# Sample states, outputs and attention scores in alternating strips of the TensorE array; the last LayerNorm passes of the first FFN in the retention heads

## The reference

```
x = LN1(alpha*x + 0.5*SwiGLU_1(x))
q_a,k_a,v_a,q_r,k_r,v_r,g_r,gate_a,gate_b = split(x @ w_in)
A = windowed attention (128), 8 query heads of 64 in groups of 4 on 2 kv heads, rotary, a sink for each head
R = retention, 4 heads, keys 128, values 256, in chunks of 128:
    o = ((q k^T) * decay_mask) v + (q * q_decay) S ;  S = S * chunk_decay + (k * k_decay)^T v
    group norm of o, times silu(g_r)
x = LN2(alpha*x + (sigmoid(gate_a)*(A @ w_br_attn) + sigmoid(gate_b)*(R @ w_br_ret)) @ w_o)
x = LN3(alpha*x + 0.5*SwiGLU_2(x))
```

## Time and profile before

| | |
|---|---|
| median of 3 runs | 2530.76 us (2530.70 to 2531.70) |
| profiled execution | 2532.04 us, span 2530.1 us |
| PE busy | 2465.7 us (97%) |
| DVE / ACT / POOL busy | 65% / 36% / 9% |
| mean granted clock of TensorE | 0.988 |
| first FFN | to about 745 us |
| mixer groups 0, 1, 2 | from 745, 1081 and 1412 us on |
| second FFN | from about 1766 us on |

### The profile page before, as it was taken

One profiled execution on the slowest core, in us unless ns is written; L12 is line 12 of the kernel. 1 busy time (PEld: TensorE's weight loads), 2 busy tenths in 40 slices (PEclk: granted clock), 3 DMA queues, 4 the chain that ended last, 5 costly groups with the idle time before them and its releaser, 6 DMA issues.

```text
span 2530.1 us, 31985 instructions
## 1 busy us (share of the span) xinstructions
PE 2465.7 (97%) x12781; PEld 2103.9 (83%) x12781; DVE 1656.1 (65%) x2253; ACT 903.5 (36%) x1280; POOL 239.1 (9%) x306
## 2 busy tenths in 40 slices
PE   7999999999999999999999999999799999999997
PEld 6888888887888999988989778887688888888886
DVE  5666565557886657676576755566765656565788
ACT  4222222243443337433265322272422222223344
POOL 3000000000121100040000311200300000000011
PEclk9999999999999999999999999999899999999999
DMA  4232222276444333333332435434122222226643
GB/s 139 84 119 81 100 83 97 84 232 197 150 131 125 109 108 90 108 117 109 109 105 92 136 110 163 147 99 142 55 79 101 84 95 80 99 88 227 205 146 125
DMA packets 225603, 300.22 MB, mean 119 GB/s; under 512 B 13392, under 2 KB 166272, under 8 KB 222624
## 3 DMA queue, kind: packets, MB, share of 16 engines
q1 hardware_dynamic: 211792, 240.43, 30.2%
q0 software_dynamic: 13088, 56.61, 6.0%
q10 hardware_dynamic: 576, 1.15, 0.1%
HBM read 243.94 MB, written 55.18 MB: 118 GB/s over the span
## 4 chain that ended last, share of the span: by engine, by line
PE 88%; DVE 6%; ACT 2%; issue 2%; POOL 1%; DMA 1%; SPq 0%; DVEq 0%; ACTq 0%; POOLq 0%
PE ps L1804 25%; PE ps L1805 25%; PE ps L1806 25%; PE ps L1860 2%; PE ps L1859 2%; PE ps L2204 1%; PE ps L1940 1%; PE ps L1941 1%; PE ps L1868 1%; DVE w_lo L445 1%; PE ps L2099 1%; PE ps L2226 1%; PE ps L2105 1%; DVE b_lo L1253 1%; ACT w_hi L439 1%
## 5 line engine op out<-in xcount | busy, mean ns | idle before, releaser
L1804 PE MATMUL ps<-xc_hi,u_hi 128*128 128x512 f32 x1232 | 484.2, 393 | 0.0
L1805 PE MATMUL ps<-xc_lo,u_hi 128*128 128x512 f32 x1232 | 481.5, 391 | 0.0
L1806 PE MATMUL ps<-xc_hi,u_lo 128*128 128x512 f32 x1232 | 480.9, 390 | 0.0
L445 DVE TENSOR_TENSOR w_lo<-raw,w_hi 128x1024 fp32r<-128x1024 f32 x198 | 253.8, 1295 | 138.9 <-ACT w_hi L439 138.7
L1806 PEld LDWEIGHTS ps<-xc_hi,u_lo 128*128 128x128 f32 x1232 | 232.1, 188 | 49.5
L1804 PEld LDWEIGHTS ps<-xc_hi,u_hi 128*128 128x128 f32 x1232 | 232.6, 189 | 46.1
L1805 PEld LDWEIGHTS ps<-xc_lo,u_hi 128*128 128x128 f32 x1232 | 232.6, 189 | 45.2
L439 ACT ACTIVATE w_hi<-raw 128x1024 fp32r<-128x1024 f32 x198 | 205.6, 1054 | 170.1 <-PE ps L1806 146.6
L1804 PE MATMUL ps<-w_hi,xg_hi 128*128 128x512 f32 (+1 forms) x720 | 247.0, 343 | 1.7 <-issue 1.7
L1804 PE MATMUL ps<-b_hi,h_hi 128*128 128x512 f32 x616 | 241.8, 393 | 3.0 <-DVE b_lo L1253 3.0
L1805 PE MATMUL ps<-w_lo,xg_hi 128*128 128x512 f32 (+1 forms) x720 | 242.6, 337 | 0.0
(11 more groups left out here) (289 smaller groups left out, 4512.6 us busy)
## 6 DMA issues: line engine op xcount, KB each, us to landing
raw<-in_w_in SPq DMA_DIRECT2D x90, 512.0 KB, 3.8
wa<-in_ffn_wi SPq DMA_DIRECT2D x88, 512.0 KB, 3.5
h_raw<-h_spill SPq DMA_DIRECT2D x154, 256.0 KB, 2.8
h_spill<-tm POOLq DMA_DIRECT2D x22, 1024.0 KB, 4.1
b_raw<-in_ffn_wo SPq DMA_DIRECT2D x66, 256.0 KB, 3.8
raw<-in_w_in SPq DMA_DIRECT2D x96, 128.0 KB, 2.3
raw<-in_w_in SPq DMA_DIRECT2D x48, 256.0 KB, 3.0
raw<-in_w_br_ret SPq DMA_DIRECT2D x24, 512.0 KB, 3.4
```

Of the source, the lines that this page charges most:

```text
L445: nc.vector.tensor_tensor(wslot(n, True), raw[:, s * D:(s + 1) * D], fr(wslot(n, False)), ALU.subtract).then_inc(lo_ready, 1)
L1804: mm(out, a_hi, b_hi, start=first, stop=False)
L1805: mm(out, a_hi, b_lo, start=False, stop=False)
L1806: return mm(out, a_lo, b_hi, start=False, stop=last)
```

## The change

1. AS: a unit is now (token tile, half h of the query heads): 2 query heads of each kv head. Its 4 matmuls alternate between rows 0 to 63 (kv head 0, bank 3) and rows 64 to 127 (kv head 1, bank 4) of the array. The sinks are ordered to fit. AV's matmuls are ordered so that neighbours write the two halves of the partitions.
2. PVQ of the sample: qT_m has 4 copies instead of 8 (copy j keeps sequences j and j + 4). L2105 becomes 8 matmuls with 32 columns of weights each, alternating between PSUM partitions 0 to 31 (sequence j) and 32 to 63 (sequence j + 4).
3. SUa, SUb: kdec_m has 4 copies, made by one instruction. Each half is 4 matmuls with K = 32 rows, alternating between rows 0 to 31 (sequences 0 to 3, bank 6) and rows 32 to 63 (sequences 4 to 7, bank 7). The halves are now sequences 0, 1, 4, 5 and 2, 3, 6, 7, and the update of `st` reads and writes in that order.
4. The scale and shift of tiles 8, 4, 5 ahead of the mixer loop and of 6 and 7 in it are gone from there; DVE does tiles 8 and 4 at P 1, tiles 5 and 6 at P 2 and tile 7 at P 3 of group 0, behind the w_lo of that step and ahead of its rope.

```diff
@@ units_of
-    return [(t, n) for t in range(3 if G < NG - 1 else 2) for n in range(HKV)]
+    return [(t, h) for t in range(3 if G < NG - 1 else 2) for h in range(GQ // 2)]
@@ DVE, behind FFN 1
-            for t in (NT - 1, 4):
-                affine_scale(0, t)
-                affine_shift(0, t)
             pace.upto(MSLOTS + 1)
-            affine_scale(0, 5)
-            affine_shift(0, 5)
@@ DVE, mixer loop, behind pace.stage(n, k)
-                if G == 0 and kind == "G" and x == 1:
-                    affine_scale(0, 6)
-                elif G == 0 and kind == "G" and x == 2:
-                    affine_shift(0, 6)
-                elif G == 0 and kind == "G" and x == 3:
-                    affine_scale(0, 7)
-                elif G == 0 and kind == "GB" and x == 0:
-                    affine_shift(0, 7)
+                if G == 0 and (kind, x) in (("P", 1), ("P", 2), ("P", 3)):
+                    for t in ((NT - 1, 4), (5, 6), (7,))[x - 1]:
+                        affine_scale(0, t)
+                        affine_shift(0, t)
@@ DVE, PVQ
-                        for half in range(2):
-                            tt(kdec_m[0:SR, half * 4 * DK:(half + 1) * 4 * DK].rearrange("p (b c) -> p b c", b=4),
...
+                        tt(kdec_m[0:SR, 0:4 * DK].rearrange("p (b c) -> p b c", b=4),
...
@@ DVE, SUa and SUb
-                    sl = st[:, half * 4 * DV:(half + 1) * 4 * DV]
+                    sl = st[:].rearrange("p (r h c) -> p h r c", r=2, h=2)[:, half]
...
@@ PE, PVQ
-                            for b in range(DB):
-                                ins = mm(out, qT_m[:, b * SR:(b + 1) * SR], st[:, b * DV:(b + 1) * DV], start=False, stop=(b == DB - 1))
+                            for j in range(4):
+                                for r in range(2):
+                                    b, cols = 4 * r + j, j * SR + 32 * r
+                                    ins = mm(out[32 * r:32 * r + 32], qT_m[:, cols:cols + 32], st[:, b * DV:(b + 1) * DV],
+                                             start=False, stop=(j == 3))
@@ PE, SUa and SUb
-                    for b in range(4):
-                        kb = (4 * half + b) * DK
-                        ins = mm(ps[:, 6 * BANK + b * DV:6 * BANK + (b + 1) * DV], kdec_m[0:SR, kb:kb + DK],
-                                 v_r[0:SR, vb + 2 * DV:vb + 3 * DV], start=True, stop=True)
+                    for b in range(2):
+                        kb = (2 * half + b) * DK
+                        for r in range(2):
+                            rows = slice(32 * r, 32 * r + 32)
+                            ins = mm(bank(6 + r, P, b * DV, DV), kdec_m[rows, kb:kb + DK], v_r[rows, vb + 2 * DV:vb + 3 * DV],
+                                     start=True, stop=True)
@@ PE, AS
-                    for q in range(GQ):
-                        ins = mm(ps[:, 3 * BANK + q * 256:3 * BANK + (q + 1) * 256],
-                                 qaT[pr, t * 512 + q * P:t * 512 + (q + 1) * P], kaT[pr, t * P:(t + 2) * P], start=True, stop=True)
+                    for par in range(2):
+                        for nkv in range(HKV):
+                            pr = slice(nkv * HD, (nkv + 1) * HD)
+                            q = 2 * h + par
+                            ins = mm(bank(3 + nkv, P, par * 256, 256), qaT[pr, t * 512 + q * P:t * 512 + (q + 1) * P],
+                                     kaT[pr, t * P:(t + 2) * P], start=True, stop=True)
@@ PE, AV
-                    for q in range(GQ):
-                        r0 = (q % 2) * HD
...
+                    for nkv in range(HKV):
                         for s in range(2):
...
+                            for par in range(2):
...
```

More of the change, by code:

```diff
@@ L1559, in _ @@
                     dve.wait_ge(qkT_ready, 2 * g + 1)
-                    tt(qT_m[:].rearrange("p (b c) -> p b c", b=DB),
-                       qT[:, 2 * P:2 * P + SR].unsqueeze(1).to_broadcast([P, DB, SR]),
-                       batch_cols[:].rearrange("p (b c) -> p b c", b=DB), ALU.mult).then_inc(qTm_ready, 1)
+                    tt(qT_m[:, 0:4 * SR].rearrange("p (b c) -> p b c", b=4),
+                       qT[:, 2 * P:2 * P + SR].unsqueeze(1).to_broadcast([P, 4, SR]),
+                       batch_cols[:, 0:4 * SR].rearrange("p (b c) -> p b c", b=4), ALU.mult).then_inc(qTm_ready, 1)
                 elif kind == "SKV":
@@ L1597, in _ @@
                         dve.wait_ge(kdec_ready, g + 1)
-                        for half in range(2):
-                            tt(kdec_m[0:SR, half * 4 * DK:(half + 1) * 4 * DK].rearrange("p (b c) -> p b c", b=4),
-                               kdec[0:SR, (3 * (g % 2) + 2) * DK:(3 * (g % 2) + 3) * DK].unsqueeze(1).to_broadcast([SR, 4, DK]),
-                               batch_rows[0:SR, 4 * half:4 * half + 4].unsqueeze(2).to_broadcast([SR, 4, DK]),
-                               ALU.mult).then_inc(kdm_ready, 1)
+                        tt(kdec_m[0:SR, 0:4 * DK].rearrange("p (b c) -> p b c", b=4),
+                           kdec[0:SR, (3 * (g % 2) + 2) * DK:(3 * (g % 2) + 3) * DK].unsqueeze(1).to_broadcast([SR, 4, DK]),
+                           batch_rows[0:SR, 0:4].unsqueeze(2).to_broadcast([SR, 4, DK]), ALU.mult).then_inc(kdm_ready, 2)
                     dve.wait_ge(o_ready, g + 1)
@@ L1696, in _ @@
                     if kind == "AS":
-                        t, nkv = units_of(G)[x]
+                        t, h = units_of(G)[x]
                         msk = att_mask[:, 256:512] if (G or t) else att_mask[:, 0:256]
@@ L2216, in _ @@
                 elif kind == "AV":
-                    t, nkv = units_of(G)[x]
+                    t, h = units_of(G)[x]
                     u = len(units_of(0)) * G + x
                     pe.wait_ge(pT_ready, u + 1)
-                    if nkv == 0 and 3 * G + t:
+                    if h == 0 and 3 * G + t:
                         pe.wait_ge(oa_lo_ready, 3 * G + t)
-                    for q in range(GQ):
-                        r0 = (q % 2) * HD
-                        out = ps[r0:r0 + HD, 2 * BANK + (2 * nkv + q // 2) * P:2 * BANK + (2 * nkv + q // 2 + 1) * P]
+                    for nkv in range(HKV):
                         for s in range(2):
-                            ins = mm(out, va[:, (t + s) * P + nkv * HD:(t + s) * P + (nkv + 1) * HD],
-                                     probT[:, (2 * q + s) * P:(2 * q + s + 1) * P], start=(s == 0), stop=(s == 1))
+                            for par in range(2):
+                                j = 2 * nkv + par
+                                out = ps[par * HD:(par + 1) * HD, 2 * BANK + (2 * nkv + h) * P:2 * BANK + (2 * nkv + h + 1) * P]
+                                ins = mm(out, va[:, (t + s) * P + nkv * HD:(t + s) * P + (nkv + 1) * HD],
+                                         probT[:, (2 * j + s) * P:(2 * j + s + 1) * P], start=(s == 0), stop=(s == 1))
                     ins.then_inc(av_done, 1)
@@ L2381, in shape_constants @@
     c["att_mask_s"] = ms.reshape(P, 384).astype(f4)
-    onehot = (b[None, :] == np.arange(DB)[:, None]).astype(f4)
-    c["batch_cols"] = np.ascontiguousarray(np.broadcast_to(onehot.reshape(1, -1), (P, DB * SR)))
-    c["batch_rows"] = np.ascontiguousarray(onehot.T)
+    onehot = (b[None, :] % 4 == np.arange(4)[:, None]).astype(f4)
+    c["batch_cols"] = np.ascontiguousarray(np.broadcast_to(onehot.reshape(1, -1), (P, 4 * SR)))
+    c["batch_rows"] = np.ascontiguousarray(np.tile((b[:, None] % 4 == np.arange(4)[None, :]).astype(f4), (1, 2)))
     return c
@@ L2409 @@
     sk = np.asarray(inputs["attn_sinks"])[0]
-    consts["sinks"] = np.ascontiguousarray(np.broadcast_to(sk[None, :], (P, HQ)))
+    by_unit = sk.reshape(HKV, GQ // 2, 2).transpose(1, 0, 2).reshape(1, HQ)
+    consts["sinks"] = np.ascontiguousarray(np.broadcast_to(by_unit, (P, HQ)))
     consts["sinks_s"] = np.ascontiguousarray(np.tile(np.repeat(sk.reshape(HKV, GQ).T, DT, axis=0), (4, 1)))
```

6 lines of the change are left out of this document (3 added, 3 removed).

## The result

The changed kernel takes 2506.88 us (median of 4 runs, 2506.64 to 2511.54), the kernel before 2530.73 us beside it: 0.9906 of it, 95% interval 0.9894 to 0.9919, 23.9 us less. Timed once more beside other runs of before it was 0.9910 (0.9895 to 0.9925). The forecast was 13.0 us less, 2517.8, with a range from 2506 to 2526.

The account below looks back on a forecast made before the run. TensorE, busy 97% of the span, was taken to bound the kernel. Retention minus 12.6, attention minus 7.2, LayerNorm passes net plus 1.7 and clock plus 5.1 gave minus 13.0 us: 2530.8 to 2517.8, range 2506 to 2526.

Parts of the forecast that it names:

- Strips of rows and columns overlap two at a time: On PE, AS and SU go from 8 steps to 4, minus 0.84 us; L2105 from 16 to 8, minus 1.68 us.
- (b): Rival: strict program order, only one matmul's second record overlaps its neighbour's first; 2521 us, chance 0.08.
- (c): Rival: row strips don't overlap when weights are 128 wide, column strips do; AS and SU give nothing; 2529 us, chance 0.06.
- (d): Rival: no strip overlaps in these shapes; 2536 us, chance 0.03.
- Retention: Last group's sample outputs and state update: 13.4 us saved, less 0.84 us that becomes SUb 3's wait; minus 12.6 us.
- Attention: AS strips in three groups: ACT takes over as bound, so minus 7.2 us of 13.4 stays.
- LayerNorm passes, first half: Six DVE passes leave the place ahead of the first rope: minus 4.2 us of wait, minus 1.7 of clock; minus 5.9 us.
- LayerNorm passes, second half: Passes ahead of rope in P 1 to P 3 delay TR, T 0 and racc; plus 7.6 us, bounds 0 and 10.
- the old places ... give nothing back: Tile 6's and 7's passes lay beside POOL's rstd, 1.51 us of DVE's wait; leaving there gains nothing.
- Clock: Half clock behind new or longer waits of PE: plus 5.1 us, bounds 0 and 12.
- the seven waits: New or longer waits of 1.3 us and more: TR 1, TR 2, B 0, AV 0 in three groups, SUb 3.
- Rival (a): ACT doesn't bound AS, DVE hides the passes, no clock is lost; 2499 us, chance 0.09.

Follow-up runs that it names:

- e5: The changed kernel with the same strips, but the matmuls of one strip issued together instead of in turn; 2512.59 us, 0.9929 of before.
- e2: The kernel before with only the retention's sample state and sample outputs in alternating strips; 2517.48 us, 0.9943 of before.
- e3: The kernel before with only the attention scores, and the order of the attention outputs, in alternating strips; 2525.44 us, 0.9975 of before.
- e6: The changed kernel with the gates' sigmoid computed from tanh on ACT, so table loads leave its rounds; 2507.61 us, 0.9907 of before.
- e13: The changed kernel with each group's first copy of probT ahead of the exponentials of unit 1 on ACT; 2522.34 us, 0.9959 of before.
- e1: The kernel before with only the ten LayerNorm passes moved into P 1, P 2 and P 3; 2530.04 us, 0.9994 of before.
- e4: The changed kernel with its ten LayerNorm passes between the w_lo copies of P instead of ahead of the rope; 2503.25 us, 0.9887 of before.
- e9: The changed kernel with tanh gates, LayerNorm passes in the gaps of P, and one gate moved ahead of AV; 2498.74 us, 0.9873 of before.
- e7: The changed kernel with 8, 10 and 13 idle DVE multiplications ahead of the rope of heads 1, 2 and 3 of the second group; 2536.63 us.

## Why the prediction was right, and where not

It was faster by 23.9 us where 13.0 were forecast: inside the range, but 0.9 us above its low end, and the error lies nearly all in one direction. The strips and the first half of the LayerNorm move did what was forecast; the price of the clock was wrong. By its steps:

- **Strips of rows and columns overlap two at a time: right.** Forecast for AS and SU groups 1.1 us, measured 1.14 and 1.13; for the sample outputs 1.9, measured 1.92. No strict turn is needed: right for groups of two (e5), wrong for four. The rivals (b), (c) and (d) fall by e2, e3 and e5.
- **Retention: right.** -12.6 forecast, -12.9 in both e2 and the whole. SKV 1's wait stayed at 1.41, SUb 3's went to 1.50 us (0.62 + 0.84 = 1.46 by the sum).
- **Attention: nearly right in size, half right in cause.** The prediction had AV 0, 1, 2 and 3 earlier by 1.3, 2.1, 2.5 and 3.2 us; counted from AS 0 they are by 1.34, 2.12, 2.72 and 3.50, and the stretch gave 3.6 in each of two groups instead of 3.2 and 1.0 instead of 0.84 in the third. ACT has 7.55 us of work a round, as forecast (es at 980.50, 988.45 and 995.60), but taking 2.56 us of it away (e6) gave 0.2 us a group. Of the 1.4 us that probT holds PE in group 0, 1.14 is AV 0's, made by the DVE and ACT loop of the softmax (e6, e13). The longest wait for probT is 2.48 us, in the last group, where the prediction allowed 1.6.
- **LayerNorm passes, first half: right.** TR 0 and the clock behind it: -5.9 forecast, 5.2 us measured by TR 1. 3.56 us are less wait (4.2 forecast; 1.45 us stay instead of 0.8), and 1.5 are clock (TR 0 to TR 1 takes 31.46 us before, and 31.39 with 1.46 of wait in it after).
- **LayerNorm passes, second half: too dear.** +7.6 us forecast, +5.0 measured: TR 1 1.46 and TR 2 1.48 (1.6 each, right), T 0 some 0.4 (1.0), B 0 1.2 (2.1), B 1 0.4 (1.3). The step that failed is "the old places ... give nothing back". They lay beside POOL's reciprocal root, and it ran slower there. Timelines of DVE and POOL, head 1, in the kernel before, and of POOL in the changed one:

```profile
803.16 1.22 DVE L1184 TENSOR_TENSOR y<-y,ln_g_down 128x1024 f32<-128x1024 f32 x1
803.42 2.43 POOL L775 TENSOR_TENSOR gn_cols<-gn_cols,neg_half 128x1 f32<-128x1 f32 x3
```

```profile
799.20 1.61 POOL L775 TENSOR_TENSOR gn_cols<-gn_cols,neg_half 128x1 f32<-128x1 f32 x3
```

  From the rope's start to GN it is 10.77 us before (795.12 to 805.89) and 9.93 after (790.91 to 800.84): the 0.82 us, which T 0, B 0 and B 1 each got. e1 and e4 have 1.61 us too. In the first two groups of the kernel before, the changed kernel and e4, these operations take 2.4 us wherever a pass or a w_lo of DVE runs beside their start, and 1.6 us where none does. So B 0's and B 1's waits came out at 1.60 and 0.87 us instead of 2.5 and 1.8.
- **Clock: wrong.** +5.1 us forecast, 0 in the profiled execution. "I take three of them to cost 1.7 us" took its rate from two waits of before; of the waits at TR 1 and TR 2, B 0, the AVs of the first groups and SUb 3 one of 54 at most had half clock behind it, and one in two that of the last group's AV. By these counts some 0.7 of the seven waits has half clock behind it, at 1.5 us each 1 us on average. That was the largest error.
- **Not in the sum: 3.6 us in the FFNs.** One profiled execution as the base put its own scatter on the result. Against the second profile of before, with its span of 2528.9 us, the change gives 23.8, of which 1.4 lie in the FFNs and 4.6 instead of 3.7 between P 0 and TR 0. So 1 us of the LayerNorm's gain is as uncertain as the rest of the scatter.

Together: 13.0 + 5.1 (clock) + 3.1 and 0.5 (FFNs) + 2.0 (passes) + 1.0 (attention) + 0.3 (retention) = 25.0 us. Rival (a), 2499, was wrong in two of its three covers (the attention has waits, DVE doesn't hide the passes), and e9 had to build them.

## What to carry to other kernels

Work put ahead of a step that others wait for delays this step by nearly its whole length, however idle its engine is over the span (rope of head 1: 4.1 us later for 4.7 us of passes); in the gaps where this engine waits between paced copies it costs nothing (e4 against the change). When one engine's time shrinks, look also for a loop that goes through two other engines, and not for the busiest one alone, and cover its latency with independent matmuls (e9). Take a base for a sum from two profiles, and price a wait in clock from how often it was followed by half clock, not from one case.

## What the runs showed of the hardware

- Matmuls of another strip overtake, by three records: two and two issued in a block are as fast as in turn (1.14 us), four and four get half of the gain (2.81 between 1.92 and 3.67).
- DVE and POOL slow each other. POOL's three small operations take 2.43 us beside a DVE multiplication of two SBUF operands and 1.61 without. Beside POOL's LayerNorm a w_lo took 2.71 us in e7 and 2.70 in the changed kernel, which is 1.23 elsewhere, and POOL's passes there 3.2 to 3.4 instead of 2.4 us. The Trainium skill, "GPSIMD Engine Reference", section "1. Specifications", names this contention for DVE instructions with two SBUF inputs; the rows agree.
- A change of ACT's table costs 1.28 us here: the load at 979.20 us is followed by the exponential at 980.50, with no drain to be seen, where the Trainium skill, "ScalarE: Activation LUTs", section "What ACT_TABLE_LOAD costs", has 2.66 us for the two. Timeline of ACT in the changed kernel:

```profile
979.20 1.28 ACT L1071 ACT_TABLE_LOAD   x1
980.50 0.20 ACT L1071 ACTIVATE es<-esd 128x4 f32<-128x4 f32 x1
```

- The half clock behind these waits lasted 3.4 or 6.8 us; 3.4 us cost 1.2 to 1.5 us of PE's time, and the same wait has it in one execution and not in the next.
